# A ConvFFN elementwise chain whose intermediates move from SBUF to PSUM, with the Gelu table loaded ahead of its loop

## The reference, cut to what matters

```python
h2 = rms_norm(x, p['norm2_g'])
a, b = jnp.split(h2 @ p['w_up'], 2, axis=-1)
a_seq = jnp.concatenate([conv_buf.astype(a.dtype), a], axis=1)
c = p['conv_b'] + sum(a_seq[:, j:j + L] * conv_w[j] for j in range(CONV_W))
x = x + (jax.nn.gelu(c) * b) @ p['w_down']
new_buf = a_seq[:, a_seq.shape[1] - (CONV_W - 1):]
```

## Time and profile before

| what | us |
| --- | --- |
| median of 3 runs | 1437.05 |
| lowest and highest run | 1435.72, 1437.99 |
| span of the profiled execution, first to last instruction | 1425.8 |
| PE busy in it | 1301.5 (91%) |
| DVE busy | 837.2 (59%) |
| POOL busy | 714.2 (50%) |
| ACT busy | 582.5 (41%) |

### The profile page before, as it was taken

The page is one execution under the profiler, slowest core; times in us unless marked ns, Lnnn a source line. Parts: engine busy times, 40 slices in busy tenths (PEclk is TensorE's granted clock), DMA queues, the critical chain, the costliest instruction groups (busy, mean ns, idle before and its releaser), DMA issues.

```text
span 1425.8 us, 24778 instructions
## 1 busy us (share of the span) xinstructions
PE 1301.5 (91%) x8240; PEld 1233.4 (87%) x8240; DVE 837.2 (59%) x1247; ACT 582.5 (41%) x951; POOL 714.2 (50%) x298
## 2 busy tenths in 40 slices
PE   3999998999999889988978999899999988899886
PEld 3799887999999879988968988899999988898885
DVE  4543328654776775378453541546749587726874
ACT  5472224433444544333444532324443545533342
POOL 2653324444666556655655343434446655566553
PEclk9999999999999999999989999999999999999998
DMA  7435333332444333433554444324334433344342
GB/s 288 148 120 191 133 106 128 117 115 91 149 147 135 116 117 128 152 120 117 178 176 142 148 148 144 111 90 135 124 115 148 141 126 104 117 148 148 103 145 74
DMA packets 53364, 191.90 MB, mean 135 GB/s; under 512 B 6048, under 2 KB 7328, under 8 KB 52896
## 3 DMA queue, kind: packets, MB, share of 16 engines
q1 hardware_dynamic: 43632, 159.15, 32.8%
q10 hardware_dynamic: 9648, 31.60, 6.2%
HBM read 182.20 MB, written 8.53 MB: 134 GB/s over the span
## 4 chain that ended last, share of the span: by engine, by line
PE 62%; DVE 21%; issue 7%; ACT 5%; POOL 2%; DMA 1%; DVEq 1%; ACTq 1%; SPq 0%; POOLq 0%
PE bank L989 27%; PE bank L958 18%; PE bank L1002 6%; DVE ol L913 5%; DVE arena L901 3%; DVE arena L902 3%; DVE arena L904 3%; ACT whi L267 2%; PE bank L1183 2%; POOL wlo L231 2%; DMA raw<-w 1%; PE bank L1086 1%; PE bank L1073 1%; DVE arena L896 1%; ACT oh L554 1%
## 5 line engine op out<-in xcount | busy, mean ns | idle before, releaser
L231 POOL TENSOR_TENSOR wlo<-raw,whi 128x1024 fp32r<-128x1024 f32 x292 | 709.3, 2430 | 668.7 <-PE bank L989 338.6
L267 ACT ACTIVATE whi<-raw 128x1024 fp32r<-128x1024 f32 x294 | 308.1, 1051 | 216.7 <-PE bank L958 91.3
L958 PE MATMUL bank<-hh,whi 128*128 128x320 f32 x832 | 266.7, 321 | 50.6 <-ACT whi L267 50.2
L989 PE MATMUL bank<-oh,whi 128*128 128x320 f32 x848 | 286.3, 338 | 19.6 <-DVE arena L754 8.9
L989 PE MATMUL bank<-ol,whi 128*128 128x320 f32 x848 | 283.5, 334 | 0.0
L989 PE MATMUL bank<-oh,wlo 128*128 128x320 f32 x848 | 282.8, 333 | 0.0
L958 PE MATMUL bank<-hl,whi 128*128 128x320 f32 x832 | 263.9, 317 | 0.0
L958 PE MATMUL bank<-hh,wlo 128*128 128x320 f32 x832 | 263.6, 317 | 0.0
L958 PEld LDWEIGHTS bank<-hh,whi 128*128 128x128 f32 x832 | 162.2, 195 | 58.6 <-ACT whi L267 56.9
L989 PEld LDWEIGHTS bank<-oh,whi 128*128 128x128 f32 x848 | 167.1, 197 | 27.4 <-issue 15.5
L989 PEld LDWEIGHTS bank<-oh,wlo 128*128 128x128 f32 x848 | 167.1, 197 | 3.4 <-issue 1.1
(11 more groups left out here) (192 smaller groups left out, 1875.3 us busy)
## 6 DMA issues: line engine op xcount, KB each, us to landing
raw<-w SPq DMA_DIRECT2D x296, 512.0 KB, 3.3
arena<-cache_k ACTq DMA_DIRECT2D x16, 512.0 KB, 5.2
arena<-cache_v ACTq DMA_DIRECT2D x16, 512.0 KB, 4.3
arena<-st_in ACTq DMA_DIRECT2D x8, 512.0 KB, 5.0
sst_out<-arena ACTq DMA_DIRECT2D x8, 512.0 KB, 2.7
arena<-mem_in ACTq DMA_DIRECT2D x2, 1024.0 KB, 6.2
con<-consts SPq DMA_DIRECT2D x1, 1288.0 KB, 13.1
x<-x_in SPq DMA_DIRECT2D x2, 640.0 KB, 9.2
```

The lines of the kernel that those rows point to most:

```text
L231: pool.tensor_tensor(out=wlo[:, s % 2, :], in0=raw[:, s, :], in1=whi[:, s, :].bitcast(f32), op=ALU.subtract).then_inc(lo_ready, 1)
L267: nc.scalar.activation(whi[:, s, :], raw[:, s, :], ACT.Copy).then_inc(hi_ready, 1)
L958: r = MM(out, a, b, start=first and i == 0, stop=last and i == 2, skip_group_check=True)
L989: r = MM(o, a, b[:, k, 0:n], start=k == 0 and i == 0, stop=k == KT_ - 1 and i == 2, skip_group_check=True)
```

## The change

The convolution is formed in one PSUM bank for each s, in place, instead of three SBUF buffers: B[0:2] in the first half, C in the second, which are the banks that `ups` of that half leaves idle. `b` is scaled in place in its own PSUM bank, and so is its product with the Gelu; ACT and the low half read the product there. `cc`, `ff` and `tb` go. Since the product now lies in the bank that PE would write next, PE waits for `fl_ready` of the tile two before it, where it waited for `f_ready`; and since `downs` writes the banks that hold the convolution, it first waits for all Gelus of its half. The Gelu's activation table is loaded by an instruction of its own ahead of the first loop.

```diff
-        cc = [[at(o_g + 700 + (3 * i + k) * 340, 340) for k in range(3)] for i in range(2)]
-        gg = [at(o_g + 2800 + i * 340, 340) for i in range(2)]
-        ff, tb = at(o_g + 3500, 2, T), at(o_g + 3500 + 2 * T, 2, T)
+        gg = [at(o_g + 700 + i * 340, 340) for i in range(2)]
...
                 rms(B[3], lv * 2 + 3)
+                nc.scalar.preload_act_table(ACT.Gelu_apprx_tanh)
...
-                            nc.scalar.activation(gg[s][:, 0:336], cc[s][2][:, 0:336], ACT.Gelu_apprx_tanh).then_inc(g_ready, 1)
+                            nc.scalar.activation(gg[s][:, 0:336], conv[s][:, 0:336], ACT.Gelu_apprx_tanh).then_inc(g_ready, 1)
...
-                            nc.scalar.activation(oh[:, i * 2 + s, :], ff[:, s, :], ACT.Copy).then_inc(fh_ready, 1)
+                            nc.scalar.activation(oh[:, i * 2 + s, :], banks[2 * s + 1][:, 0:T], ACT.Copy).then_inc(fh_ready, 1)
...
+            dve.sem_inc(fl_ready, 8)
...
-                            lk(V.tensor_scalar(cc[s][0][:, 0:336], apad[s][:, 0:336], cw(0), par[:, bass.ds(jw + C_CB, 1)], ALU.mult, ALU.add), 5 * s + 2)
-                            lk(V.scalar_tensor_tensor(out=cc[s][1][:, 0:336], in0=apad[s][:, 1:337], scalar=cw(1), in1=cc[s][0][:, 0:336],
-                                                      op0=ALU.mult, op1=ALU.add), 5 * s + 3)
-                            V.scalar_tensor_tensor(out=cc[s][2][:, 0:336], in0=apad[s][:, 2:338], scalar=cw(2), in1=cc[s][1][:, 0:336],
-                                                   op0=ALU.mult, op1=ALU.add).then_inc(c_ready, 1)
+                            cv = conv[s][:, 0:336]
+                            lk(V.tensor_scalar(cv, apad[s][:, 0:336], cw(0), par[:, bass.ds(jw + C_CB, 1)], ALU.mult, ALU.add), 5 * s + 2)
+                            lk(V.scalar_tensor_tensor(out=cv, in0=apad[s][:, 1:337], scalar=cw(1), in1=cv, op0=ALU.mult, op1=ALU.add), 5 * s + 3)
+                            V.scalar_tensor_tensor(out=cv, in0=apad[s][:, 2:338], scalar=cw(2), in1=cv, op0=ALU.mult, op1=ALU.add).then_inc(c_ready, 1)
...
-                            lk(V.tensor_tensor(out=tb[:, s, :], in0=bb[:, 0:T], in1=rs[:, :], op=ALU.mult), 5 * s + 4)
+                            lk(V.tensor_tensor(out=bb[:, 0:T], in0=bb[:, 0:T], in1=rs[:, :], op=ALU.mult), 5 * s + 4)
...
-                            lk(V.tensor_tensor(out=ff[:, s, 0:SEQ], in0=gg[s][:, 0:SEQ], in1=tb[:, s, 0:SEQ], op=ALU.mult), 5 * s + 5)
-                            V.tensor_tensor(out=batches(ff[:, s, SEQ:T]), in0=batches(gg[s][:, 258:338])[:, :, 0:8], in1=batches(tb[:, s, SEQ:T]),
+                            lk(V.tensor_tensor(out=bb[:, 0:SEQ], in0=gg[s][:, 0:SEQ], in1=bb[:, 0:SEQ], op=ALU.mult), 5 * s + 5)
+                            V.tensor_tensor(out=batches(bb[:, SEQ:T]), in0=batches(gg[s][:, 258:338])[:, :, 0:8], in1=batches(bb[:, SEQ:T]),
                                             op=ALU.mult).then_inc(f_ready, 1)
...
-                            V.tensor_tensor(out=ol[:, i * 2 + s, :], in0=ff[:, s, :], in1=oh[:, i * 2 + s, :].bitcast(f32),
+                            V.tensor_tensor(out=ol[:, i * 2 + s, :], in0=bb[:, 0:T], in1=oh[:, i * 2 + s, :].bitcast(f32),
                                             op=ALU.subtract).then_inc(fl_ready, 1)
...
-                    pe.wait_ge(f_ready, lv * FT + i * 2 + (j0 + s - 1 + 8))
+                    pe.wait_ge(fl_ready, lv * FT + i * 2 + (j0 + s - 1 + 8))
...
                     u = u0
+                    pe.wait_ge(g_ready, lv * FT + j0 + n)
                     for q in range(2):
                         for i in range(n // 2):
-                            pe.wait_ge(fl_ready, lv * FT + j0 + 2 * i + 2) if q == 0 else None
+                            pe.wait_ge(fl_ready, lv * FT + j0 + 2 * i + 2 + 8) if q == 0 else None
```

More of the change, by code:

```diff
@@ L533, in _, with ups @@
                 rms(B[3], lv * 2 + 3)
-                def ups(u0, n, j0):
+                nc.scalar.preload_act_table(ACT.Gelu_apprx_tanh)
+                def ups(u0, n, j0, banks, conv):
                     with act.Fori(0, n // 2) as i:
@@ L553, in ups @@
                             act.wait_ge(f_ready, lv * FT + i * 2 + (j0 + s + 1) + 8)
-                            nc.scalar.activation(oh[:, i * 2 + s, :], ff[:, s, :], ACT.Copy).then_inc(fh_ready, 1)
-                ups(U_UP1, FA, 0)
+                            nc.scalar.activation(oh[:, i * 2 + s, :], banks[2 * s + 1][:, 0:T], ACT.Copy).then_inc(fh_ready, 1)
+                AC = [A[0], A[1], C[0], C[1]]
+                ups(U_UP1, FA, 0, AC, B[0:2])
                 for u in range(U_DN1, U_UP2):
@@ L559, in _ @@
                     hi(u + 4)
-                ups(U_UP2, FB, FA)
+                ups(U_UP2, FB, FA, B, C)
                 act.wait_ge(fh_ready, lv * FT + FT)
@@ L880, in _, with ups @@
                     link(V.memset(apad[s][:, 0:2], 0.0))
-                def ups(j0, n, banks, u0):
+                def ups(j0, n, banks, conv, u0):
                     base = dve_n[0]
@@ L911, in ups @@
                                             op=ALU.mult).then_inc(f_ready, 1)
                             dve.wait_ge(fh_ready, lv * FT + i * 2 + (j0 + s + 1))
-                            V.tensor_tensor(out=ol[:, i * 2 + s, :], in0=ff[:, s, :], in1=oh[:, i * 2 + s, :].bitcast(f32),
+                            V.tensor_tensor(out=ol[:, i * 2 + s, :], in0=bb[:, 0:T], in1=oh[:, i * 2 + s, :].bitcast(f32),
                                             op=ALU.subtract).then_inc(fl_ready, 1)
-                            dve.wait_ge(fl_ready, lv * FT + i * 2 + (j0 + s + 1))
+                            dve.wait_ge(fl_ready, lv * FT + i * 2 + (j0 + s + 1 + 8))
@@ L928, in _ @@
                 AC = [A[0], A[1], C[0], C[1]]
-                ups(0, FA, AC, U_UP1)
+                ups(0, FA, AC, B[0:2], U_UP1)
                 downs(U_DN1 + 6, U_UP2, [B, AC], False)
-                ups(FA, FB, B, U_UP2)
+                ups(FA, FB, B, C, U_UP2)
                 downs(U_DN2 + 5, UNITS, [AC, B], True)
@@ L1295, in downs @@
                     u = u0
+                    pe.wait_ge(g_ready, lv * FT + j0 + n)
                     for q in range(2):
                         for i in range(n // 2):
-                            pe.wait_ge(fl_ready, lv * FT + j0 + 2 * i + 2) if q == 0 else None
+                            pe.wait_ge(fl_ready, lv * FT + j0 + 2 * i + 2 + 8) if q == 0 else None
                             if q == 1 and i == 0:
-                                pe.wait_ge(fl_ready, lv * FT + j0 + n)
+                                pe.wait_ge(fl_ready, lv * FT + j0 + n + 8)
                             ready(u)
```

## The result

| what | before | after |
| --- | --- | --- |
| median, us | 1436.38 (4 runs, 1431.10 to 1437.99) | 1355.24 (4 runs, 1349.93 to 1359.21) |
| ratio of the times, 95% interval | | 0.9448 [0.9414, 0.9481] |
| span of the profiled execution | 1425.8 | 1353.6 |
| ConvFFN, both layers | 548.9 | 469.6 |

The account below looks back on a forecast made before the run. DVE, held by POOL's subtractions, was taken to set the pace of `ups`; freed, PE bounds the ConvFFN at 235.2 us a layer, saving 78.4: 1425.8 - 78.4 = 1347.4, plus 11.25 gives 1358.6 us, range 1353 to 1390.

Parts of the forecast that it names:

- main step: In `ups`, L902, L904, L909 and L913 read one tensor from a bank and run unheld: 0.57, 0.57, 0.42, 0.48 us.
- as cheap as to SBUF: DVE's writes to PSUM were taken at the cost of SBUF writes, since reading PSUM costs nothing (484 against 480 ns).
- the first rival: In `ups`, only L913 is freed and lines writing to PSUM stay held: 1394 us, chance 0.11.
- the two values of the prediction: L901, with one SBUF input: about 0.46 us if freed, near 1.3 if one SBUF input is enough to be held.
- the tile may grow by over 1 us before it matters: DVE's tile in `ups`, put at 5.43 us against PE's 7.09, has over 1 us of room.
- the clock's part: The ConvFFN's share of clock not granted, 3% of 274, 8 us, was counted as going with PE's holes.
- the cross-check: Layer one's ConvFFN: waits of 28.5 us and 8 us of clock give 36.7, near the 38.8 forecast to fall away.
- cover of 4.4 us: PE's wait for `fl_ready` in `ups` costs nothing: tile through after 6.2 us, bank wanted after 10.6.
- cover of 0.2 us: The wait for all Gelus ahead of `downs` costs nothing: last Gelu at 3.3 us, PE's second unit 3.5.
- The second rival: PSUM frees nothing, and the wait ahead of `downs` adds 7.1 us four times, 28.5: 1465 us, chance 0.05.
- The table loads: In the ConvFFN loops 24 loads of 1.283 us go and two come: nothing by themselves, as ACT idles.
- the carried 11.25: Added to the forecast span of 1347.4 us, as the old median lay 11.25 above the old span: 1358.6 us.

Follow-up runs that it names:

- the small subtraction: The kernel before, with POOL subtracting only 8 of each weight unit's 1024 columns and no DVE operand moved: 1311.46 us, ratio 0.9151.
- the convolution alone: The kernel before, with only the convolution in PSUM and the wait for all Gelus; the product stays in SBUF: 1403.77 us, ratio 0.9783.
- Two more multiplications: The changed kernel with two further DVE multiplications of a bank by an SBUF tensor in each tile, ahead of L913: 1352.68 us, ratio 0.9451.
- four more: The changed kernel with four further DVE multiplications of a bank by an SBUF tensor in each tile, ahead of L913: 1375.54 us, ratio 0.9607.
- the product alone: The kernel before, with only `b` and its product in PSUM and the wait for `fl_ready`; convolution in SBUF: 1381.2 us, ratio 0.9619.

## Why the prediction was right

*The cause and the place.* That DVE set the pace because POOL's subtraction held it was read from timelines alone; the small subtraction showed it without moving an operand. One reading there was loose: L904 is said to have run where POOL was idle, but its last 0.34 us, to 498.35, lie inside the subtraction from 498.01. It had begun first and took its free 0.57 us; that subtraction took 2.62 us where the other took 2.38. The prediction's main step, that every line which reads one of its tensors from a bank is as free as L907, held line by line: 571 to 575 ns for L904 and L905 where 0.57 was taken, 429 for L909 (0.42 taken) and 492 for L913 (0.48 taken). The prediction took "as cheap as to SBUF" for writes to PSUM, of which no row had told; in the rows it is 4 or 5 ns for L904, L905 and L909 (569 and 424 in the run with the small subtraction) and 8 to 16 for L907 (500, against a median of 492 in that run and 484 in the kernel before). This is the step that kept the first rival out.

*L901.* Neither of the two values of the prediction came, 0.46 us free or 1.29 held, but 630 ns, always. It isn't held, yet it is 176 ns longer than the 454 that the run with the small subtraction gives for the same line into SBUF, and the convolution alone gives 630 as well: it is the bank as output, and nothing around it. By the rule that the prediction took from the Trainium skill, SBUF — State Buffer, section "Who interferes with whom", the line was held for its mode, and a PSUM output ends that; the trace agrees (629 to 634 ns in 44 cases), and shows the other side of it, that the faster mode goes as well. The Trainium skill, VectorE: DVE Perf Modes, section "Why PSUM operands drop a tier", says that any PSUM operand keeps a float32 instruction at the plain rate. Its reason is about reading; the trace shows the same where the bank is only the output. An estimate by that page's clock of 0.96 GHz, with one element a cycle in place of two, is 336 / 2 / 0.96 = 175 ns, against the 176 measured. In the sum it cost nothing: a tile of 5.4 + 0.2 = 5.6 us, the step measured without the turn of the loop, is far under PE's.

*DVE's tile against PE's.* PE's step came out at 7.05 us, 0.04 under the 7.09 taken. The turn of the loop, which the prediction could not read and left to the room of 1.6 us, takes 0.5 in every second tile, so that 1.2 us are left on average. Two more multiplications, 0.65 us, fitted; with four more the mean tile was 7.28 us and the room was used up. So the claim "the tile may grow by over 1 us before it matters" holds, and its end lies close behind.

*The ConvFFN.* 235.2 us a layer forecast, 235.10 and 234.54 measured. That the clock's part goes with the holes held: 1.00 in both windows. That part is larger than the 8 us of the cross-check: PE's busy time for the same 1588 matmuls fell from 245.31 to 233.74 us in layer one, by 11.6.

*The waits.* `fl_ready` in place of `f_ready` cost nothing: in the ConvFFN's list of PE's waits none for it, or for DVE inside `ups`, is left. Its cover of 4.4 us lasts only while DVE's tile is under PE's: with the product alone the tile is longer, and the same wait takes 21.7 us over the whole run. The wait for all Gelus was put at nothing, with a cover of 0.2 us and the remark that behind it all lag is charged; it took 0.3 us at most (L903's longer time is 0.17 of what the cover lacked), and the experiments showed the rest: 8.0 us a time on the kernel before, 7.2 on the convolution alone, 3.8 with a tile 0.23 us too long. The second rival, with that wait on an unchanged DVE, was priced at 7.1 a time and 28.5 together; measured, its wait costs 32.7 us of ConvFFN. Its mechanism is real and its condition did not occur. The table loads at nothing: confirmed from both sides.

*The total.* Here two terms were off and cancelled. The prediction carried 11.25 us from the old span to the median. Most of that is no fixed cost: in the 13 later runs of the kernel before, each with its span listed, the time stands 2.2 to 3.3 us above it, and in the changed kernel's profiled execution 1355.84 - 1353.6 = 2.2. So the execution with a span of 1425.8 was one of the faster ones (1424.6 to 1436.9 in the 13). In the other direction the rest of the program, which the change doesn't touch, took 441.18 + 427.83 and the end, 884.0 us, in the profile after, and 876.9 in that of before; in the stretch ahead of the second ConvFFN it took 427.83 at a granted clock of 0.94. The same stretch of the kernel before, in the windows view:

```profile
712.98:1136.05 423.07, 402.06 (x2531) 375.06 (x2531) 230.14 (x390) 169.84 (x270) 198.17 (x82) 0.96 0.39 135
```

It has the same instructions, at a clock of 0.96 and 4.8 us shorter. The forecast of the span, 1347.4, was so 6.2 us short: 7.1 by the rest of the program, less 0.9 by the ConvFFN. The median came within 3.4 us because the carried 11.25 stood in for a spread that both kernels have around their fastest execution. Of the four executions of the changed kernel the fastest had a span of 1347.5, the one profiled 1353.6. What makes one execution some us longer than another in these stretches stays open.

## What to carry to other kernels

If an instruction on VectorE has a mean far above its shortest case, or, like L913 here, above that of a like instruction, lay its timeline beside GpSimd's: cases that end just behind a GpSimd instruction are held by it, and one of their two SBUF inputs moved to PSUM frees them, at a few ns each (a `tensor_scalar` into PSUM lost 0.18 us). Free all of the lines in the loop, since holds that end at one line can come back at the next, and count how much the loop may still grow before the next engine's pace, because a wait that collects a whole loop (here for all Gelus) charges the whole lag at once, and the half clock behind it. Measure such a change by the window of its stage in the profile; it repeated within 0.6 us here where totals moved by some us.

## What the runs showed of the hardware that was not expected

- `tensor_scalar` on 128 x 336 float32 takes 454 ns from SBUF to SBUF and 630 from SBUF to PSUM, while `scalar_tensor_tensor` of the same size takes 569 with both inputs and the output in SBUF, and 573 with an input and the output in PSUM.
- Of four DVE instructions of 0.48 us each that don't depend on each other, one starts every 0.40 us (four in 1.68 us).
- After 3.8 us without a matmul PE ran at 1.2 GHz for 5.6 us, 21 matmuls at 0.267 us, before it came back to 2.4 GHz (0.145 us a matmul); after the waits of 0.3 us in the changed kernel the windows stay at a granted clock of 1.00.
- Holds move: with L909 and L913 freed, the mean of the third convolution step rose from 1014 to 1653 ns.
